# The delta-rule loop of the third block: dense operands of two heads above each other, and 64x64 tiles in place of block-diagonal 128x128 products

## The reference

```
def wkv7_scan(r, w, k, v, a, b):          # each (B, S, 8 heads, 64)
    def step(state, inp):                 # state: (B, 8, 64, 64) from zeros
        r_t, w_t, k_t, v_t, a_t, b_t = inp
        sa = einsum('bhij,bhj->bhi', state, a_t)
        state = (state * w_t[:, :, None, :] + sa[..., None] * b_t[:, :, None, :]
                 + v_t[..., None] * k_t[:, :, None, :])
        return state, einsum('bhij,bhj->bhi', state, r_t)
```

## Time and profile before

| | |
|---|---|
| median of three runs | 4563.32 us (4549.02 to 4565.37) |
| span of the profiled execution | 4563.6 us |
| the profiled execution's own time | given only as its span |
| TensorE (PE) busy | 4427.4 us, 97% |
| TensorE weight loads (PEld) busy | 2387.4 us, 52% |
| VectorE (DVE) busy | 1772.2 us, 39% |
| ScalarE (ACT) busy | 900.7 us, 20% |
| GpSimd (POOL) busy | 852.0 us, 19% |
| the loop's first product starts | 3240.26 us |
| the loop's last result is out | 3610.3 us |

### The profile page before, as it was taken

One profiled execution on the slowest core, in us unless ns is written; L12 is line 12 of the kernel. 1 busy time (PEld: TensorE's weight loads), 2 busy tenths in 40 slices (PEclk: granted clock), 3 DMA queues, 4 the chain that ended last, 5 costly groups with the idle time before them and its releaser, 6 DMA issues.

```text
span 4563.6 us, 37880 instructions
## 1 busy us (share of the span) xinstructions
PE 4427.4 (97%) x15188; PEld 2387.4 (52%) x15188; DVE 1772.2 (39%) x2821; ACT 900.7 (20%) x1603; POOL 852.0 (19%) x656
## 2 busy tenths in 40 slices
PE   8999999999999999999999999899999999999999
PEld 4467444444444456654444445644699744444444
DVE  4635463333325123333996403534333332222311
ACT  2114120000002122221332112431244310000000
POOL 5212042423201100000552000000111003222310
PEclk9989999999999999999999999999999999999999
DMA  4420101111111110001111111010000121111121
GB/s 188 157 82 1 37 28 37 46 46 46 37 46 65 37 72 12 10 19 37 37 37 46 56 46 37 19 49 28 14 1 1 56 92 42 41 46 46 66 75 44
DMA packets 52605, 215.45 MB, mean 47 GB/s; under 512 B 5856, under 2 KB 7392, under 8 KB 50512
## 3 DMA queue, kind: packets, MB, share of 16 engines
q1 hardware_dynamic: 47808, 168.58, 10.5%
q0 software_dynamic: 4624, 44.45, 2.5%
HBM read 194.13 MB, written 18.87 MB: 47 GB/s over the span
## 4 chain that ended last, share of the span: by engine, by line
PE 91%; DVE 4%; POOL 1%; ACT 1%; issue 1%; DMA 1%; SPq 0%; DVEq 0%; POOLq 0%; ACTq 0%
PE bank L474 30%; PE bank L183 28%; PE bank L2554 7%; PE bank L2741 4%; PE bank L1700 2%; PE bank L1753 2%; PE bank L2752 1%; PE bank L1736 1%; PE bank L2482 1%; PE bank L1739 1%; PE bank L2501 1%; PE bank L2581 1%; PE bank L1716 1%; PE bank L2730 1%; PE bank L2682 1%
## 5 line engine op out<-in xcount | busy, mean ns | idle before, releaser
L183 PE MATMUL bank<-H,ring 128*128 128x512 f32 x1920 | 835.2, 596 | 10.6 <-ACT H L371 4.7
L183 PEld LDWEIGHTS bank<-H,ring 128*128 128x128 f32 x1920 | 366.1, 191 | 469.9 <-issue 454.2
L183 PE MATMUL bank<-ABC,ring 128*128 128x512 f32 x1200 | 520.1, 594 | 2.5 <-POOL ABC L1654 2.0
L183 PEld LDWEIGHTS bank<-ABC,ring 128*128 128x128 f32 x1200 | 226.7, 190 | 286.4 <-issue 278.0
L474 PE MATMUL bank<-H,ring 128*128 128x512 f32 x736 | 323.5, 593 | 0.8 <-ACT ABC L1799 0.8
L2067 DVE SCALAR_TENSOR_TENSOR bank<-ABC,params,bank 128x1024 f32<-128x1024 f32 x184 | 237.3, 1290 | 8.0
L474 PEld LDWEIGHTS bank<-H,ring 128*128 128x128 f32 x736 | 140.0, 190 | 176.9 <-issue 176.9
L474 PE MATMUL bank<-H,X 128*128 128x512 f32 x400 | 179.9, 593 | 0.4 <-POOL H L825 0.4
L474 PE MATMUL bank<-X 128*128 128x512 f32 x400 | 179.8, 593 | 0.0
L474 PE MATMUL bank<-X,ring 128*128 128x512 f32 x368 | 165.4, 593 | 0.0
L1639 POOL TENSOR_TENSOR ABC<-ABC 128x1024 f32<-128x1024 f32 x48 | 113.3, 2361 | 220.4 <-ACT ABC L1873 214.4
(11 more groups left out here) (548 smaller groups left out, 6780.8 us busy)
## 6 DMA issues: line engine op xcount, KB each, us to landing
ABC<-in_ada SPq DMA_DIRECT2D x48, 512.0 KB, 5.7
ring<-in_gu SPq DMA_DIRECT2D x44, 512.0 KB, 4.2
ring<-in_up SPq DMA_DIRECT2D x32, 512.0 KB, 4.0
ring<-in_down SPq DMA_DIRECT2D x32, 512.0 KB, 4.1
ring<-in_conv_in SPq DMA_DIRECT2D x24, 512.0 KB, 4.2
ring<-in_ffn SPq DMA_DIRECT2D x16, 704.0 KB, 5.3
ring<-in_proj SPq DMA_DIRECT2D x16, 512.0 KB, 5.9
ring<-in_mix SPq DMA_DIRECT2D x16, 512.0 KB, 4.4
```

The lines of the kernel that those rows point to most:

```text
L183: mm = nc.tensor.matmul(bank[:, 2 * (m % 2) + h, :], ring[:, s % RING, k * P:(k + 1) * P], rhs(k)[:, h * HALF:(h + 1) * HALF], start=(k == ...
```

## The change

Each operand now is dense: [128 partitions, 4 groups, 64 columns], the head pair's two 64x64 matrices above each other. `product` makes eight matmuls where it made four: for each group one on partitions 0 to 63 and one on 64 to 127, both into the same bank, each a 64x64 tile of the array. All ScalarE and VectorE operations have 256 columns instead of 512 (`t_r` keeps 512). Besides:

- `turned` is no transpose any more, but a product with a 64x64 identity for each half; the transposes of the inverse at levels 1 to 4 (`turn_inv`) become products (`level_inv_t`), and stand behind `level_inv`.
- GpSimd's staging copies, their semaphore and the zeroing of X go; TensorE reads a, b, k and v where they are. Only the state is set to zero, after `rw3` is done.
- All slots lie in H. SyncE's wait for the end of the loop goes, and X's first half comes back from DRAM at the loop's start. GpSimd's four multiplications for the bonus stand at the loop's start.
- The masks have 64 columns each, with an identity among them, that ScalarE uses for its identities; so ScalarE now waits for the masks' DMA, and that DMA for the end of VectorE's preparation, as TensorE does.

The core of the diff (semaphore lists, slot tables and the masks' making are left out):

```
-            def product(b, lhs, rhs, at=0, width=P, start=True, stop=True):
+            pe.wait_ge(*prep_dve.all())
+            halves = [slice(0, 64), slice(64, 128)]
+
+            def product(b, lhs, rhs, width=L, start=True, stop=True):
                 for q in range(4):
-                    mm = nc.tensor.matmul(bank[:, b, at + q * width:at + q * width + width], lhs[:, q, :], rhs(q),
-                                          start=start and (q == 0 or stop), stop=stop, skip_group_check=True)
+                    for rows in halves:
+                        mm = nc.tensor.matmul(bank[rows, b, q * width:(q + 1) * width], lhs(q)[rows], rhs(q)[rows],
+                                              start=start and (q == 0 or stop), stop=stop, skip_group_check=True)
                 return mm
...
             def turned(b, src):
                 for q in range(4):
-                    mm = nc.tensor.transpose(bank[:, b, q * P:(q + 1) * P], src[:, q, :], ident[:, :])
+                    for rows in halves:
+                        mm = nc.tensor.matmul(bank[rows, b, q * L:(q + 1) * L], src(q)[rows], ident[rows, rows],
+                                              start=True, stop=True, skip_group_check=True)
                 return mm
...
                     level_x(4, c1, 3)
-                    turn_inv(3, c1, 5)
...
-                    pe.wait_ge(*rw_pool.after(0, f"stage{c2}"))
...
-                    product(2, a_bd[c2 % 3], tokens(b_, c2), width=L)
-                    product(0, b_bd, queries_and_a(c2))
-                    product(1, k_bd, queries_and_a(c2)).then_inc(*rw_pe.did(f"gram{c2}"))
+                    product(2, tokens(a_, c2), tokens(b_, c2))
+                    product(0, tokens(b_, c2), queries_and_a(c2), width=2 * L)
+                    product(1, tokens(k_, c2), queries_and_a(c2), width=2 * L).then_inc(*rw_pe.did(f"gram{c2}"))
                 if 0 <= c1 < NCH:
...
                     level_inv(4, c1, 4)
+                    level_inv_t(4, c1, 5)
...
-                    nc.vector.tensor_tensor(state, state, decay_last[:, :, c:c + 1].broadcast_to([P, 4, P]),
+                    nc.vector.tensor_tensor(state, state, decay_last[:, :, c:c + 1].broadcast_to([P, 4, L]),
                                             ALU.mult).then_inc(*rw_dve.did(f"state{c}"))
```

GpSimd's part after it:

```
+            pool.wait_ge(*prep_dve.all())
+            pool.dma_start(kept[:, 0:15 * L], io["rwkv_masks"]).then_inc(masks_landed, 16)
+            pool.wait_ge(*taken("rw3"))
+            pool.memset(state, 0.0).then_inc(*rw_zero.did("zeroed"))
+            pool.dma_start(norm_room[:, 0:9 * P], io["pair_const"]).then_inc(lnx_landed, 16)
+            pool.wait_ge(x_spilled, 16)
+            pool.dma_start(X[:, 0:4, :], x_kept[:, 0:4, :]).then_inc(x_back, 16)
```

More of the change, by code:

```diff
@@ L2199, in build @@
             LEVELS = 5
[L2200 to L2205, removed]
-            x_in = u_
[L2207 to L2213, removed]
+            slots = [Hf[:, at * 4 * L:(at + 1) * 4 * L].rearrange("p (q n) -> p q n", q=4) for at in range(26)]
+            wide_slots = [Hf[:, at * 4 * L:(at + 2) * 4 * L].rearrange("p (q n) -> p q n", q=4) for at in (26, 28, 30)]
+            t_r = wide_slots
+            t_ak, b_tok, k_tok, v_tok3, inv_t = (slots[at:at + 3] for at in (0, 3, 6, 9, 12))
+            t_ab, inv = slots[15:17], slots[17:19]
+            x_lev, state, u_ = [None] + slots[19:24], slots[24], slots[25]
+            x_in = u_
+            mask_rows = lambda t, n: t[:, n * L:(n + 1) * L]
+            strict, causal_r, eye = (mask_rows(kept, n) for n in (0, 1, 14))
+            over_q = lambda m: m.unsqueeze(1).broadcast_to([P, 4, L])
+            bank_q = lambda b: bank[:, b, 0:4 * L].rearrange("p (q n) -> p q n", q=4)
+            bank_pairs = lambda b: bank[:, b, :].rearrange("p (q z t) -> p q z t", q=4, z=2)
             rw_zero = steps("rwkv_zero", "zeroed")
@@ L2331, in b3_gpsimd @@
             pool.dma_start(kept[:, 0:9 * P], io["pair_const"]).then_inc(rwkv_landed, 16)
-            pool.wait_ge(*prep_dve.after(0, "bf3"))
-            pool.memset(Xf[:, 0:7 * 512], 0.0).then_inc(*rw_zero.did("zeroed"))
             pool.wait_ge(*prep_pe.all())
[L2335 to L2354, removed]
@@ L2356, in b3_gpsimd @@
+            for m in range(4):
+                pool.wait_ge(*prep_act.after(0, f"sum{m}"))
+                nc.gpsimd.tensor_tensor(bonus[:, m, :], bonus[:, m, :], v_[:, m, :], ALU.mult).then_inc(*prep_pool.did(f"bonus{m}"))
+            pool.wait_ge(*rw_pe.after(0, f"bk_turn{NCH - 1}"))
             pool.wait_ge(mix_spilled, 16)
             pool.dma_start(C[:, 0:4, :], attention_kept).then_inc(mix_back, 16)
-            pool.wait_ge(*rw_pe.all())
-            pool.wait_ge(*rw_dve.all())
-            pool.wait_ge(x_spilled, 16)
@@ L2592, in b3_tensor @@
                         pe.wait_ge(*rw_act.after(0, f"out{c - 1}"))
-                    product(6, t_ak[c % 3], whole(v_tok3[c % 3]), stop=False)
-                    product(7, v_tok3[c % 3], lambda q: t_r[c % 3][:, q, L:2 * L], width=L, stop=False)
+                    product(6, whole(t_ak[c % 3]), whole(v_tok3[c % 3]), stop=False)
+                    product(7, whole(v_tok3[c % 3]), lambda q: t_r[c % 3][:, q, L:2 * L], stop=False)
                     if c:
                         pe.wait_ge(*rw_dve.after(0, f"state{c - 1}"))
-                    product(6, a_bd[c % 3], whole(state), start=False).then_inc(*rw_pe.did(f"x_in{c}"))
-                    product(7, state, tokens(r_, c), width=L, start=False, stop=False)
+                    product(6, tokens(a_, c), whole(state), start=False).then_inc(*rw_pe.did(f"x_in{c}"))
+                    product(7, whole(state), tokens(r_, c), start=False, stop=False)
                 if 0 <= c1 < NCH:
@@ L2609, in b3_tensor @@
                     pe.wait_ge(*rw_act.after(0, f"x_in{c}"))
-                    product(6, inv_t[c % 3], whole(x_in)).then_inc(*rw_pe.did(f"u{c}"))
+                    product(6, whole(inv_t[c % 3]), whole(x_in)).then_inc(*rw_pe.did(f"u{c}"))
                 if 0 <= c1 < NCH:
@@ L2613, in b3_tensor @@
                     pe.wait_ge(*rw_dve.after(0, f"x3_{c1}"))
-                    pe.wait_ge(*rw_act.after(0, f"inv_t2_{c1}"))
                     level_inv(3, c1, 4)
+                    level_inv_t(3, c1, 5)
                 if 0 <= c < NCH - 1:
                     pe.wait_ge(*rw_act.after(0, f"u{c}"))
-                    product(6, k_tok[c % 3], whole(v_tok3[c % 3]), stop=False)
-                    product(6, b_tok[c % 3], whole(u_), start=False).then_inc(*rw_pe.did(f"state{c}"))
+                    product(6, whole(k_tok[c % 3]), whole(v_tok3[c % 3]), stop=False)
+                    product(6, whole(b_tok[c % 3]), whole(u_), start=False).then_inc(*rw_pe.did(f"state{c}"))
                 if 0 <= c1 < NCH:
@@ L2634, in b3_tensor @@
                     level_inv(4, c1, 4)
+                    level_inv_t(4, c1, 5)
                 if c >= 0:
                     pe.wait_ge(*rw_act.after(0, f"u{c}"))
-                    product(7, u_, lambda q: t_r[c % 3][:, q, 0:L], width=L, start=False).then_inc(*rw_pe.did(f"out{c}"))
+                    product(7, whole(u_), lambda q: t_r[c % 3][:, q, 0:L], start=False).then_inc(*rw_pe.did(f"out{c}"))
                 if c2 < NCH:
@@ L2910, in b3_scalar @@
             for n in range(1, LEVELS + 1):
-                last = nc.scalar.activation(x_lev[n], over_q(ident[:, :]), ACT.Identity)
+                last = nc.scalar.activation(x_lev[n], over_q(eye), ACT.Identity)
             last.then_inc(*rw_act.did("eye"))
```

79 lines of the change are left out of this document (31 added, 48 removed), and 6 rows, old and new, of the table rw_pe.

## The result

The changed kernel takes 4429.19 us (median of four runs, 4423.68 to 4434.33) against 4558.19 us (four runs, 4549.02 to 4565.37): ratio 0.9715, 95% interval 0.9697 to 0.9734, so 2.85% or 129 us faster. Timed once more beside each other, four runs against seven, the two gave 4434.18 and 4555.41 us, 121 us (ratio 0.9728, 0.9714 to 0.9743).

The account below looks back on a forecast made before the run. TensorE's instruction issue was taken as the bound; the loop was to fall from 370 to 261 us (214 full iterations, 47 edges), so 4563 - 109 + 5 = 4460 us, range 4435 to 4650, the forecast's own 4435 to 4515.

Parts of the forecast that it names:

- The bound: Whole kernel: TensorE busy 97% of the span; the loop, 370 us, is TensorE's instruction issue at 112 ns each.
- Price of a tile's instruction: Loop products on 64x64 tiles: 30 ns per instruction, 56 ns for wide ones; 227 us of work in the loop.
- bound (a): Loop's TensorE instructions: weight load half as long and two halves working at the same time, 28 ns each; taken as 30.
- Rival A2: Loop: the halves overlap only in part, 40 ns per instruction; loop 321 us, total 4514; chance 0.16.
- B: Loop: the two halves take turns, 57 ns per instruction; loop 450 us, total 4643, slower; chance 0.25.
- C: Loop: weight loads have a fixed length, 112 ns, without overlap; total 4990; chance 0.07 including worse.
- Waits in a period: Full loop iteration: TensorE waits 0.25 us before inv3 and 0.75 before inv1, 1.0 us together; period 15.3 us.
- The edges: Loop's first and last iterations: 58 us before, 39 of it work; forecast 27 work plus 19 to 20 waits, 47.
- The 5 us "for small waits not seen": Forecast total: 5 us added for small waits not seen in the hand count.
- The frame: Starting level of the sum: profiled execution's 4563.6 us, taken as equal to the median of 4563.3.
- Edits at nothing: GpSimd's copies taken out, SyncE's earlier weights and the earlier X: no gain, as TensorE waits for no DMA behind the loop.
- Rival D: Loop near break-even, from a pace of 45 to 50 ns or a falling clock; about 4563 +-20; chance 0.07.

Follow-up runs that it names:

- e3: Changed kernel with both halves of each loop product reading operands from partitions 0 to 63, so the result is not the whole one; 4599.58 us.

## Why the prediction was right in kind and short in size

**The bound.** Right: the loop is TensorE's issue, and what goes there shows in the whole: 129.8 us in the loop of the first traces, 127 in that of the second, 129 and 121 us in the medians, which the clock ahead of the loop moves by several us.

**Price of a tile's instruction (bound (a), 30 ns; wide 56).** Right, a little high: 13.88 = 416 x 0.0292 + 32 x 0.054. The two inputs hold: half as long for half the columns (58 ns for one tile against 112), and two tiles at once. Rival A2 (40 ns), B (57 ns, turns) and C (fixed length) fall by the pace of 29 ns. Even the kernel made to approach B, with the halves apart, came to 36 ns, for a reason that no rival of the prediction had: TensorE starts matmuls of the other tile ahead of their turn. The bank rule of the Trainium skill ("TensorEngine Tiling (Array Packing)", "Restrictions and Gotchas") would have given B; here both tiles wrote one bank in each product at 29 ns, on different partitions of it, and the measurement decides. What the Trainium skill says on that page under "Key Properties", that different tiles work in parallel, agrees with the trace.

**Waits in a period (1.0 us).** Right in place, both behind VectorE; 0.72 in size. With the price, a period came out at 15.3 where it was 14.6: 14 x 0.65 = 9 us of the miss.

**The edges.** This is the step that failed: "the waits, which are of latency and partly at half clock, I leave at 19 to 20: 47". The edges are what lies ahead of the first and behind the last update of the state. First and last part of the loop, before and then after:

```profile
3240.26:3285.05 44.79, 39.41 (x289) 37.33 (x290) 12.53 (x20) 17.36 (x32) 9.01 (x18) 0.85 0.05 14
3596.78:3610.20 13.42, 10.83 (x90) 10.01 (x87) 2.05 (x3) 4.24 (x8) 0.01 (x1) 1.00 0.00 1
3228.17:3255.02 26.85, 23.58 (x696) 22.51 (x698) 7.70 (x19) 11.88 (x34) 10.22 (x6) 1.00 0.33 129
3460.08:3468.30 8.22, 5.99 (x176) 5.53 (x176) 1.21 (x3) 2.37 (x7) 0.00 (x0) 1.00 0.03 10
```

They took 58 us before and 35 after, not 47: 12 us of the miss. Two things were wrong. The first is a count: "of which 39 is work" should be 3120 - 14 x 196 = 376 instructions of 0.112 us, 42 us, so only 16 us were left to carry over. The second is that they were carried over whole. After the change 26 or 27 of the 35 us are instructions, and 8 to 9 us remain of the 16. TensorE's idle time fell from 8.0 to 5.5 us, about in proportion to the operations of ScalarE and VectorE that I had made shorter by a third one paragraph earlier. The other 5 us or so lie in TensorE's pace: the half clock, 13.7 us long in both traces of before, was absent or 3.4 us after. If everything costs double at half clock, it cost up to 6.9 us before, an estimate; no run separates it.

**The 5 us "for small waits not seen".** No such waits showed: the period has the two that were forecast. It was a surcharge without a row.

**The frame.** The sum was made against the profiled execution, whose span is 4563.6; a run's time is about 2.0 us over its span (4423.68 and 4421.7 after), so it was the slowest of the three runs, 4565.37, while the median of before with more runs is 4558 and 4555. 4460 - 9 - 12 - 5 - 5 = 4429. Of the 26 us by which the gain was larger than forecast, 21 lie in the loop and 5 in the surcharge. The 5 us of the frame move only the level, and are no more than what two medians of the changed kernel differ by (4429 and 4434).

**Edits at nothing.** Right, as far as tested: the earlier streams and the earlier X. GpSimd's copies were not tried by themselves; TensorE's instructions and the waits above account for the loop without them. The entry gained 0.6 us (TensorE waited 2.6 instead of 3.2 us), as forecast about 0.5.

**Rival D, the clock.** It didn't happen, but by less of a margin than its 0.07 says: e3, with all instructions but operands on one half of the partitions, took 170 us more than the changed kernel. The changed kernel, whose products use both halves, stayed at 2.4 GHz.

## What to carry to other kernels

Where small matmuls are paced by their weight loads, two 64x64 tiles on the two halves of the partitions take half of a load's length each; alternate them at least every four instructions, and keep both halves at work: with one alone the clock stayed at 1.2 GHz here. Make the sum for the loop's first and last iterations as for the middle ones, with the new durations, instead of carrying the old remainder over. Once instructions are cheap, count how many of them stand between a product and the one that needs its result: here moving three products was worth another 0.3%.

## What was not expected of the hardware

- TensorE started three matmuls of another tile ahead of program order, so that tiles in runs of four overlapped whole (29 ns) and in runs of eight in part (36 ns).
- Two tiles with the same operand partitions and different result partitions overlapped too: 53 ns per instruction with 64 moving columns against 107 ns for one tile alone, both at half clock.
- With operands on 64 of the 128 partitions, TensorE was granted 1.2 GHz for 413 to 420 us on end, of which it was busy without a gap for 358 us; on both halves, with 86% busy, 2.4 GHz. The page "TensorE: Matmul & The Clock Gate" of the Trainium skill, section "Part 1: The HAM clock gate", says that activity releases the throttle; these three runs show that a TensorE without a gap can stay at the lower level.
